# A chain of 270 weight blocks on one core: the first two blocks of a stage run on x·g, and the norm's factor is applied to their banks

## The chip, the cores and the metric

One core of a Trainium2 chip runs the whole program in one launch. The time is that of the device in microseconds (us): the median of three runs of the kernel before is 1714.77 (1704.56 to 1725.2). The engines are PE (matrix multiplication), ACT, DVE, POOL (GpSimd) and SP, which issues transfers. They run in parallel and meet at semaphores.

## The reference

Batch 1, 256 tokens, width 1024, all in fp32. Nine residual steps and two norms, each step on a normed x:

```
rmsnorm(x, g) = x * rsqrt(mean(x*x) + eps) * g
modulate(h, shift, scale) = h * (1 + scale) + shift        # shift, scale, gain from c_act @ mod_w + mod_b
swiglu(h) = (silu(h @ w_gate) * (h @ w_up)) @ w_out        # hidden width 2816
first model:  x += 0.5*swiglu(rmsnorm(x)); x += mixer_1(rmsnorm(x)); x += 0.5*swiglu(rmsnorm(x)); x = rmsnorm(x)
second model: for i in 0, 1:
    x += 0.5 * g1 * swiglu(modulate(rmsnorm(x), sh1, sc1))
    x += g2 * mixer(modulate(rmsnorm(x), sh2, sc2))        # i = 0: pool + SSD; i = 1: attention
    x += 0.5 * g3 * swiglu(modulate(rmsnorm(x), sh3, sc3))
return rmsnorm(x)
```

The mean runs over the 1024 channels of a token, so a norm needs the whole of x, while its factor is one number for each token.

## The kernel before

x is held transposed as 8 tiles of 128 channels by 256 tokens. The phases are n = 0 to 10: ffn, mix1, ffn, final norm (n = 3), ffn (4), mix2 (5), ffn (6), ffn (7), mix3 (8), ffn (9), final norm (10). All weights are one stream of 270 blocks of 128x2048 fp32 (1 MB), which SP loads into three slots in turn. ACT rounds a block to fp32r (`act_split`, L176, whi), DVE forms the remainder (`dve_split`, L184, wlo), and PE multiplies in three passes, hi by hi, lo by hi and hi by lo: 48 matmuls of 256 columns a block (`pe_in` L252, `pe_out` L284). x is treated alike: xh rounded by ACT, xl the remainder by DVE. Each slot is free again when PE has used it (semaphore w_used). F0 is a stage's first block. An ffn stage has 33 blocks: gate F0, up F0+1, then gate, up and out in turn, in loops on each engine. In the stages n = 0, 2, 4 and 6 DVE also works off the table of shifts and gains (`mod_block` L575, L578), which GpSimd loads; its sums end in a few PE matmuls before the last four output tiles of the stage (L504) and one DVE addition (L595).

Each engine does its instructions in the order in which they are written; nothing is reordered. Between two stages: DVE adds the output banks to x (`dve_residual` L304, or L309 with a gain, four pairs b = 0 to 3); ACT squares each pair (L335); DVE adds the two tiles of a pair (`dve_pair` L325); PE sums over channels with matmuls of one column (`pe_norm` L369) and runs matmuls without use between them (`pe_keep_warm` L357); ACT takes the square root (128x2, L340) and DVE the reciprocal (L391); PE spreads it over the partitions (L375); DVE forms xm = x·g·factor (`dve_norm` L401, 128x256 each, x8; in mix2 and mix3 also + shift, L398), ACT xh (L345, L347) and DVE xl (L428, L430). PE starts block F0 as soon as the first tile of xh is there (L244), the passes with xl last. The remainder of F0+1 is formed in two halves around the reciprocal (L222, L226). `post` multiplies silu(gate) by up (L532, L563, L534, L565).

## Time and profile before

| | us |
|---|---|
| median of three runs | 1714.77 |
| profiled execution, its own time | 1711.11 |
| its span (first to last instruction) | 1709.4 |
| PE busy in the span | 1675.8 |
| DVE busy | 1201.2 |
| ACT busy | 809.4 |
| POOL busy | 85.1 |

The page of the profile gives the busy time of each engine; the chain of waits follows the end of the program back, from each instruction to what released it. The mean granted clock of PE in this execution is 0.991 of full speed (2.4 GHz). Ends of matmuls are modelled, and PE counts as busy with the matmuls without use as well.

### The profile page before, as it was taken

The page shows a single profiled execution, that of the slowest core. Times are in us where ns is not written, and L with a number is a line of the kernel's source. Part 1 is how long each engine was busy: PE and PEld are TensorE (multiplying, and loading weights), DVE is VectorE, ACT ScalarE, POOL GpSimd, SP SyncE. Part 2 cuts the span into 40 slices and gives each one's busy share as a digit, 9 for nine tenths or more (in the row PEclk, how much of TensorE's full clock was granted, in tenths as well). Part 3 has the DMA queues.
Part 4 walks back from the last instruction along what each step waited for, and adds up shares of the span by engine and source line. Part 5 has one row for each costly group of instructions (what it writes and reads, how often), then busy time and mean ns, then how long its engine had stood idle before and what let it go on. Part 6 is the DMA issues. An engine that isn't in the chain of part 4 may idle for free.

```text
span 1709.4 us, 34392 instructions
## 1 busy us (share of the span) xinstructions
PE 1675.8 (98%) x14512; PEld 1641.4 (96%) x14512; DVE 1201.2 (70%) x1303; ACT 809.4 (47%) x874; POOL 85.1 (5%) x110
## 2 busy tenths in 40 slices
PE   9999999999999999999998999999999999999998
PEld 9999999999999999999997899999999988899998
DVE  5888875676788877878866778646555666764544
ACT  5444556644544344343565543435434455554342
POOL 0000000000000000000012000000000003100000
PEclk8999999999999999999999999999999999999999
DMA  7998754444498856888442368643555433345551
GB/s 311 344 340 308 265 176 171 147 150 164 176 347 325 326 214 230 318 323 304 177 149 102 122 249 320 242 175 138 208 203 189 170 123 128 126 168 191 179 196 50
DMA packets 50491, 365.08 MB, mean 214 GB/s; under 512 B 5728, under 2 KB 5856, under 8 KB 6240
## 3 DMA queue, kind: packets, MB, share of 16 engines
q1 hardware_dynamic: 39744, 287.04, 46.0%
q0 software_dynamic: 10368, 75.50, 11.9%
q8 instruction: 74, 1.21, 0.3%
q10 hardware_dynamic: 288, 1.18, 0.2%
q14 instruction: 17, 0.14, 0.0%
HBM read 362.65 MB, written 1.05 MB: 213 GB/s over the span
## 4 chain that ended last, share of the span: by engine, by line
PE 88%; DVE 7%; ACT 3%; issue 1%; DMA 0%; SPq 0%; ACTq 0%; DVEq 0%
PE bank L252 50%; PE bank L284 24%; PE bank L267 3%; PE bank L244 2%; DVE wlo L184 2%; PE bank L357 2%; PE bank L369 1%; PE bank L1661 1%; ACT whi L176 1%; DVE m_e L1923 1%; DVE m_p L1426 1%; ACT m_e L1802 0%; DVE xm L401 0%; DVE x L309 0%; PE bank L1619 0%
## 5 line engine op out<-in xcount | busy, mean ns | idle before, releaser
L184 DVE TENSOR_TENSOR wlo<-raw,whi 128x2048 fp32r<-128x2048 f32 x261 | 598.2, 2294 | 209.3 <-ACT whi L176 208.9
L252 PE MATMUL bank<-xh,whi 128*128 128x256 f32 x2608 | 729.6, 280 | 2.7 <-DVE wlo L184 1.4
L252 PE MATMUL bank<-xl,whi 128*128 128x256 f32 x2608 | 726.4, 279 | 0.0
L252 PE MATMUL bank<-xh,wlo 128*128 128x256 f32 x2608 | 726.3, 278 | 0.0
L176 ACT ACTIVATE whi<-raw 128x2048 fp32r<-128x2048 f32 x261 | 497.9, 1912 | 313.2 <-PE bank L252 187.4
L252 PEld LDWEIGHTS bank<-xh,whi 128*128 128x128 f32 x2608 | 492.2, 189 | 5.4 <-issue 2.8
L252 PEld LDWEIGHTS bank<-xh,wlo 128*128 128x128 f32 x2608 | 493.1, 189 | 0.0
L252 PEld LDWEIGHTS bank<-xl,whi 128*128 128x128 f32 x2608 | 490.4, 188 | 0.1
L284 PE MATMUL bank<-hid_hi,whi 128*128 128x256 f32 x1056 | 294.5, 279 | 0.0
L284 PE MATMUL bank<-hid_lo,whi 128*128 128x256 f32 x1056 | 294.1, 278 | 0.0
L284 PE MATMUL bank<-hid_hi,wlo 128*128 128x256 f32 x1056 | 294.1, 278 | 0.0
L284 PEld LDWEIGHTS bank<-hid_hi,wlo 128*128 128x128 f32 x1056 | 199.7, 189 | 0.0
L284 PEld LDWEIGHTS bank<-hid_hi,whi 128*128 128x128 f32 x1056 | 198.9, 188 | 0.4
L284 PEld LDWEIGHTS bank<-hid_lo,whi 128*128 128x128 f32 x1056 | 198.2, 188 | 0.0
L534 ACT ACTIVATE hid_hi<-hid 128x512 fp32r<-128x512 f32 x66 | 41.8, 633 | 283.1 <-DVE hid L563 283.1
L578 DVE SCALAR_TENSOR_TENSOR mod_acc<-mod_raw,c_act,mod_acc 128x1024 f32<-128x1024 f32 x126 | 161.6, 1282 | 2.6
L563 DVE TENSOR_TENSOR hid<-gate,bank 128x512 f32<-128x512 f32 x66 | 45.3, 686 | 81.9 <-PE bank L252 81.7
L1996 POOL DMA_DIRECT2D mod_raw<-mod_in x72 | 38.3, 532 | 937.0 <-DVE mod_acc L578 925.3
L565 DVE TENSOR_TENSOR hid_lo<-hid,hid_hi 128x512 fp32r<-128x512 f32 x66 | 45.7, 693 | 46.2 <-ACT hid_hi L534 46.2
L357 PE MATMUL bank<-ident_b 128*128 128x128 bf16 x690 | 49.5, 229 | 0.0
L357 PEld LDWEIGHTS bank<-ident_b 128*128 128x128 bf16 x690 | 46.7, 108 | 0.2
L659 DVE SCALAR_TENSOR_TENSOR m_pre<-bank,params,m_pre 128x255 f32<-128x255 f32 (+2 forms) x84 | 34.0, 474 | 14.9 <-ACT m_pre L646 14.9
(315 smaller groups left out, 1812.2 us busy)
## 6 DMA issues: line engine op xcount, KB each, us to landing
raw<-stream_in SPq DMA_DIRECT2D x270, 1024.0 KB, 4.8
mod_raw<-mod_in POOLq DMA_DIRECT2D x72, 1024.0 KB, 6.6
params<-params_in SPq DMA_DIRECT2D x1, 1474.0 KB, 16.0
x<-x_in SPq DMA_DIRECT2D x2, 512.0 KB, 4.4
...
```

Of the source, the lines that this page charges most:

```text
L176: act.activation(whi[:, s, :], raw[:, s, :], ACT.Copy).then_inc(sem("w_hi_ready"), 1)
L184: dve.tensor_tensor(wlo[:, s, :], raw[:, s, :], whi[:, s, :].bitcast(F32), ALU.subtract)\
L244: last = pe.matmul(out[:, m, :], w[:, s, c:c + P], (xh, xl)[part][:, k, :], start=(part == 0 and k == 0 and m == 0 and w is whi), stop=(pa ...
L252: last = pe.matmul(out[:, m, :], (whi, wlo)[wp][:, s, k * 256 + m * P:k * 256 + m * P + P], (xh, xl)[ap][:, k, :], start=(k == 0 and j == ...
L267: last = pe.matmul(out[:, tt, :], (xh, xl)[ap][:, k, tt * P:tt * P + P], (whi, wlo)[wp][:, s, k * 256:k * 256 + 256], start=(k == 0 and j ...
L284: mm = pe.matmul(pair(acc[d // 2])[:, d % 2, :], (whi, wlo)[wp][:, s, c:c + P], (hi, lo)[ap][:, kt, :], start=(first and d % 2 == 0 and kt ...
L357: pe.matmul(bank_[:, 0:P], ident_b[:, :], ident_b[:, :], start=True, stop=True, skip_group_check=True)
L534: act.activation(hid_hi[:, parity], hid[:, :, :], ACT.Copy).then_inc(sem("hid_rounded"), 1)
L563: dve.tensor_tensor(hid[:, :, :], gate[:, :, :], pair(UP), ALU.mult).then_inc(sem("hid_ready"), 1)
L565: dve.tensor_tensor(hid_lo[:, parity], hid[:, :, :], hid_hi[:, parity].bitcast(F32), ALU.subtract)\
L578: ins = dve.scalar_tensor_tensor(out=mod_acc[:, :], in0=mod_raw[:, s, t * D:t * D + D], scalar=c_act[:, k:k + 1], in1=mod_acc[:, :], op0=A ...
L1996: pool.dma_start(mod_raw[:, s, :], a_mod[ds(s * P + 2 * P * turn, P), :])\
```

## The change

In each of the nine stages with matmuls the first two blocks run on xg = x·g (and g·(1 + scale) where there is modulation), before the norm's factor is known. ACT rounds xg right after each pair of x (no instruction stood there before), and DVE forms its remainder between the pairs (`dve_scaled_rest`, L458 and L461). PE runs F0 and F0+1 on them (`pe_start`, L359); in the modulated stages each matmul has 258 columns: two more carry the shift. The squares are summed by GpSimd (`pool_squares`, L430 128x512 three times, L432 128x256) and by one fp32 matmul with a square of ones (L366) behind block F0; ACT takes a root of 128x256 (L413), DVE a reciprocal of 128x256 (L492). DVE then forms xm (L495), ACT xh, DVE xl (L504, L506), on which block F0+2 and all later ones run. The banks of the first two blocks are multiplied by the factor when DVE reads them (`dve_first_scaled`, L473), and the shift's column is copied first (L472). GpSimd forms the remainder of block F0+3 (`pool_split`, L448). The matmuls without use are gone but at the last norm. The norm between the models (n = 3) has no phase of its own any more: its factor and that of n = 4 are formed together in stage 4 (two ones matmuls, and GpSimd sums both sets of squares, L439), and x itself is normed late in that stage (`dve_final_inside`). A product of a pair stands one place later in the loops. SP issues half of params first, then x, the first block, consts and the next two blocks.

On DVE, from stage 6 to stage 7, the instructions before (L309 is the residual, L401 xm, L430 xl, L184 a block's remainder):

```order
L309 SCALAR_TENSOR_TENSOR x<-bank,gres,x 128x256 x2
L325 TENSOR_TENSOR xm<-xm 128x256
L457 SCALAR_TENSOR_TENSOR gmod<-mod_tab,params 128x8
L325 TENSOR_TENSOR xm<-xm 128x256
L222 TENSOR_TENSOR wlo<-raw,whi 128x1024
L391 RECIPROCAL rstd<-std 128x2
L226 TENSOR_TENSOR wlo<-raw,whi 128x1024
L401 SCALAR_TENSOR_TENSOR xm<-x,gmod,bank 128x256 x8
L423 TENSOR_SCALAR gres<-mod_tab 128x8
L430 SCALAR_TENSOR_TENSOR xl<-xm,mod_tab,xh 128x256 x8
L184 TENSOR_TENSOR wlo<-raw,whi 128x2048
L563 TENSOR_TENSOR hid<-gate,bank 128x512
```

and with the change (L288 is the residual, L461 the remainder of xg, L191 a block's remainder, L495 xm, L506 xl):

```order
L288 SCALAR_TENSOR_TENSOR x<-bank,gres,x 128x256 x2
L461 SCALAR_TENSOR_TENSOR xg_lo_a<-x,gmod,xg_hi_a 128x256 x2
L288 SCALAR_TENSOR_TENSOR x<-bank,gres,x 128x256 x2
L461 SCALAR_TENSOR_TENSOR xg_lo_a<-x,gmod,xg_hi_a 128x256 x4
L191 TENSOR_TENSOR wlo<-raw,whi 128x2048 x2
L492 RECIPROCAL rstd<-std 128x256
L495 SCALAR_TENSOR_TENSOR xm<-x,gmod,rstd 128x256 x8
L506 SCALAR_TENSOR_TENSOR xl<-xm,mod_tab,xh 128x256 x8
L513 TENSOR_SCALAR gres<-mod_tab 128x8
L609 SCALAR_TENSOR_TENSOR gmod<-mod_tab,params 128x8
L472 COPY cols<-bank 128x1
L473 TENSOR_TENSOR gate<-bank,rstd 128x256
```

The two whole remainders stand ahead of the reciprocal, which has 128x256 elements in the place of 128x2; reads of the four banks with the factor follow xl, and then the product of the first pair.

On PE, at the same place, before (L369 sums squares, L357 is the work without use, L244 the first block of stage 7):

```order
L369 MATMUL bank<-consts,xm 128x1
L357 MATMUL bank<-ident_b 128x128 x14
L369 MATMUL bank<-consts,xm 128x1 [waits x_paired]
L369 MATMUL bank<-consts,xm 128x1
L357 MATMUL bank<-ident_b 128x128 x8
L369 MATMUL bank<-consts,xm 128x1 [waits x_paired]
L369 MATMUL bank<-consts,xm 128x1
L357 MATMUL bank<-ident_b 128x128 x14
L375 MATMUL bank<-consts,rstd 128x128 [waits rstd_ready]
L375 MATMUL bank<-consts,rstd 128x128
L357 MATMUL bank<-ident_b 128x128 x26
L244 MATMUL bank<-xh,whi 128x256 [waits xn_rounded,w_lo_ready]
```

and with the change, around the matmul with ones (the rows ahead of it are the end of block F0, those behind it block F0+1):

```order
L359 MATMUL bank<-xg_hi_a,wlo 128x258 x2
L359 MATMUL bank<-xg_lo_a,whi 128x258 [waits xg_split]
L359 MATMUL bank<-xg_lo_a,whi 128x258
L366 MATMUL bank<-xm,consts 128x256 [waits squares_added]
L359 MATMUL bank<-xg_hi_a,whi 128x258 [waits w_lo_ready]
L359 MATMUL bank<-xg_hi_a,whi 128x258
L359 MATMUL bank<-xg_hi_a,wlo 128x258 x2
L359 MATMUL bank<-xg_lo_a,whi 128x258 x2
L359 MATMUL bank<-xg_hi_a,whi 128x258 x2
```

PE no longer waits for the reciprocal between the stages; it waits for GpSimd's sum of the squares between blocks F0 and F0+1.

On POOL, which before had only transfers in the ffn stages, the order of a stage is now:

```order
L2245 REGISTER_ALU
L2245 COMPARE_AND_BRANCH
L430 TENSOR_TENSOR xm<-xm 128x2x256 [waits x_squared]
L430 TENSOR_TENSOR xm<-xm 128x2x256 [waits squares_step,x_squared] x2
L432 TENSOR_TENSOR xm<-xm 128x256 [waits squares_step]
L448 TENSOR_TENSOR wlo<-raw,whi 128x2048 [waits w_lo_ready,w_hi_ready]
```

The fourth block's remainder stands behind the sums.

The diff, cut to its core:

```diff
-                if b >= 1 and n + 1 < len(phases):
-                    dve_pair(dve, n + 1, b - 1)
-            if n + 1 < len(phases):
-                dve_gain(dve, n + 1)
-                dve_pair(dve, n + 1, 3)
+                if b >= 1:
+                    dve_next_pair(dve, n, b - 1)
+            dve_next_pair(dve, n, 3)
...
+        def pe_start(pe, n):
+            F0, ni = first_block[n], split_index[n]
+            hi, lo = scaled_split(n)
+            w = width(n)
+            for b in range(2):
+                s = slot_of(F0 + b)
+                outs = [bank_[:, 0:w] for bank_ in first_banks(n)[b]]
+                pe.wait_ge(sem("w_lo_ready"), F0 + b + 1)
+                for k in range(KD):
+                    for j, (wp, ap) in enumerate(((0, 0), (1, 0), (0, 1))):
+                        if b == 0 and j == 0:
+                            pe.wait_ge(sem("xg_rounded"), 8 * ni + k + 1)
+                        if b == 0 and j == 2:
+                            pe.wait_ge(sem("xg_split"), 8 * ni + k + 1)
+                        for m in range(2):
+                            c = k * 256 + m * P
+                            last = pe.matmul(outs[m], (whi, wlo)[wp][:, s, c:c + P], (hi, lo)[ap][:, k, 0:w],
+                                             start=(k == 0 and j == 0), stop=(k == KD - 1 and j == 2), skip_group_check=True)
+                last.then_inc(sem("w_used"), 1)
+                if b == 0:
+                    if n == 0:
+                        pe.wait_ge(sem("consts_loaded"), 16)
+                    pe.wait_ge(sem("squares_added"), ni + 1)
+                    mm = pe.matmul(UP[:, 0:T], ones, xm[:, 0, :], start=True, stop=True, skip_group_check=True)
+                    if n == AFTER_FINAL:
+                        pe.wait_ge(sem("final_squares_added"), 3)
+                        mm = pe.matmul(UP[:, T:2 * T], ones, final_squares[:, 0, :], start=False, stop=True,
+                                       skip_group_check=True)
+                    mm.then_inc(sem("x_summed"), 1)
...
+            for b in range(4):
+                x_ready(act, n, b)
+                if b == 0 and shift is not None:
+                    act.activation(hi[:, :, T:W], pair_of_columns(shift), ACT.Copy)
+                for k in (2 * b, 2 * b + 1):
+                    act.activation(hi[:, k, 0:T], x[:, k, :], ACT.Identity, scale=g[:, k:k + 1]).then_inc(sem("xg_rounded"), 1)
+                if n > 0:
+                    squares(b)
...
+            act_split(act, F0 + 2)
+            act.wait_ge(sem("x_summed"), ni + 1)
...
+            act_split(act, F0 + 3)
...
+        def pool_squares(pool, n):
+            ni = split_index[n]
+            for b in range(1, 4):
+                pool.wait_ge(sem("x_squared"), 4 * ni + b + 1)
+                if b > 1:
+                    pool.wait_ge(sem("squares_step"), 3 * ni + b - 1)
+                pool.tensor_tensor(xm[:, 0:2, :], xm[:, 0:2, :], xm[:, 2 * b:2 * b + 2, :], ALU.add).then_inc(sem("squares_step"), 1)
+            pool.wait_ge(sem("squares_step"), 3 * ni + 3)
+            pool.tensor_tensor(xm[:, 0, :], xm[:, 0, :], xm[:, 1, :], ALU.add).then_inc(sem("squares_added"), 1)
+            if n == AFTER_FINAL:
+                fs = final_squares
+                pool.wait_ge(sem("final_squared"), KD)
+                for i, h in enumerate((4, 2, 1)):
+                    if i:
+                        pool.wait_ge(sem("final_squares_added"), i)
+                    pool.tensor_tensor(fs[:, 0:h, :], fs[:, 0:h, :], fs[:, h:2 * h, :], ALU.add)\
+                        .then_inc(sem("final_squares_added"), 1)
+        def pool_split(pool, n):
+            b = first_block[n] + 3
+            s = slot_of(b)
+            pool.wait_ge(sem("w_hi_ready"), b + 1)
+            pool.wait_ge(sem("w_lo_ready"), b)
+            pool.tensor_tensor(wlo[:, s, :], raw[:, s, :], whi[:, s, :].bitcast(F32), ALU.subtract)\
+                .then_inc(sem("w_lo_ready"), 1)
...
+        def dve_scaled_rest(dve, n, b):
+            ni = split_index[n]
+            hi, lo = scaled_split(n)
+            g = gain_of(n)
+            if b == 0 and n in MOD_OF:
+                dve.wait_ge(sem("xg_rounded"), 8 * ni + 1)
+                dve.tensor_tensor(lo[:, :, T:W], pair_of_columns(shift_of(n)), hi[:, :, T:W].bitcast(F32), ALU.subtract)
+            for k in (2 * b, 2 * b + 1):
+                dve.wait_ge(sem("xg_rounded"), 8 * ni + k + 1)
+                dve.scalar_tensor_tensor(out=lo[:, k, 0:T], in0=x[:, k, :], scalar=g[:, k:k + 1],
+                                         in1=hi[:, k, 0:T].bitcast(F32), op0=ALU.mult, op1=ALU.subtract)\
+                   .then_inc(sem("xg_split"), 1)
...
+        def dve_first_scaled(dve, n, b, outs):
+            F0, ni = first_block[n], split_index[n]
+            dve.wait_ge(sem("w_used"), F0 + b + 1)
+            for m in range(2):
+                bank_ = first_banks(n)[b][m]
+                if n in MOD_OF:
+                    dve.tensor_copy(cols[:, 68 + 2 * b + m:69 + 2 * b + m], bank_[:, T:T + 1])
+                dve.tensor_tensor(outs[m], bank_[:, 0:T], rstd[:, :], ALU.mult).then_inc(sem("first_scaled"), 1)
...
+            dve_split(dve, F0 + 2)
...
+            dve.reciprocal(rstd[:, :], std[:, :]).then_inc(sem("rstd_ready"), 1)
+            dve.wait_ge(sem("rstd_ready"), ni + 1)
...
+                dve.scalar_tensor_tensor(out=xm[:, k, :], in0=x[:, k, :], scalar=g[:, k:k + 1], in1=rstd[:, :],
+                                         op0=ALU.mult, op1=ALU.mult).then_inc(sem("xn_ready"), 1)
...
+            dve_gain(dve, next_stage(n))
+            dve.wait_ge(sem("w_lo_ready"), F0 + 4)
...
+            def first_post():
+                dve_first_scaled(dve, n, 0, [gate[:, m, :] for m in range(2)])
+                dve_first_scaled(dve, n, 1, [hid[:, m, :] for m in range(2)])
+                dve.wait_ge(sem("first_scaled"), 4 * split_index[n] + 4)
...
+            def turn(i, with_mod, last=False):
+                g0 = group0[f]
+                if with_mod:
+                    mod_block(0, g0, i)
+                dve_split(dve, F0 + 4, i, 6)
+                if with_mod:
+                    mod_block(1, g0, i)
+                dve_split(dve, F0 + 5, i, 6)
...
+            if n == AFTER_FINAL:
+                dve_final_inside(dve)
...
+            dve_split(dve, F0 + 34)
```

## Rows read from the trace of the kernel before

**Rows 1.** The page's first part: busy us of each engine, share of the span.
```profile
PE 1675.8 (98%) x14512; PEld 1641.4 (96%) x14512; DVE 1201.2 (70%) x1303; ACT 809.4 (47%) x874; POOL 85.1 (5%) x110
```

**Rows 2.** Busy time in the eight gaps between stages (span, then engines, granted clock, DMA).
```profile
437.98:443.43 5.45, 5.45 (x81) 5.44 (x82) 4.90 (x10) 1.88 (x5) 0.00 (x0) 1.00 0.00 0
625.20:640.82 15.62, 14.80 (x199) 14.55 (x198) 10.26 (x25) 5.22 (x12) 0.00 (x0) 0.89 0.20 69
...
1170.28:1176.27 5.99, 5.89 (x85) 5.71 (x83) 5.69 (x14) 2.24 (x5) 0.00 (x0) 1.00 0.02 3
...
sum 56.77, PE 54.63 PEld 53.42 DVE 48.77 ACT 19.24 POOL 0.00; mean PE 6.83 PEld 6.68 DVE 6.10 ACT 2.41 POOL 0.00
```

**Rows 3.** Chain of waits (start, us, what): stage 2's tables, then PE's blocks.
```profile
448.26 0.24 DVE tab_pos_f L1557
...
453.25 0.42 ACT cos L1581
...
455.64 11.32 PE bank L252 x96
...
686.20 11.31 PE bank L252 x96
...
834.37 6.91 PE bank L244 x48
```

**Rows 4.** Timeline of DVE from the end of stage 6 (last matmul 1170.28) on.
```profile
1170.71 0.87 DVE L309 SCALAR_TENSOR_TENSOR x<-bank,gres,x 128x256 f32<-128x256 f32 x2
...
1175.05 3.21 DVE L401 SCALAR_TENSOR_TENSOR xm<-x,gmod,bank 128x256 f32<-128x256 f32 x8
...
1178.25 3.25 DVE L430 SCALAR_TENSOR_TENSOR xl<-xm,mod_tab,xh 128x256 fp32r<-128x256 f32 x8
```

**Rows 5.** Groups of instructions of the whole program, by line.
```profile
L184 DVE TENSOR_TENSOR wlo<-raw,whi 128x2048 fp32r<-128x2048 f32 x261 | 598.2, 2294 | 209.3 <-ACT whi L176 208.9
...
L176 ACT ACTIVATE whi<-raw 128x2048 fp32r<-128x2048 f32 x261 | 497.9, 1912 | 313.2 <-PE bank L252 187.4
```

**Rows 6.** Timeline of DVE in mix1: a product with a bank, a reciprocal of 128x256.
```profile
292.32 0.42 DVE L980 TENSOR_TENSOR rstd<-std,bank 128x256 f32<-128x256 f32 x1 [1.20 <-ACT std L868]
292.77 1.75 DVE L982 RECIPROCAL rstd<-rstd 128x256 f32<-128x256 f32 x1
```

**Rows 7.** Timeline of POOL and DVE in mix2 (start, us; work that overlaps).
```profile
888.64 2.29 DVE L184 TENSOR_TENSOR wlo<-raw,whi 128x2048 fp32r<-128x2048 f32 x1 [1.89 <-ACT whi L176]
...
889.14 1.83 POOL L1385 COPY xm<-m_pu 128x4 f32<-128x4 f32 x1 [75.87 <-ACT m_pu L1294]
...
895.96 1.03 POOL L1386 TENSOR_TENSOR xm<-xm 128x504 f32<-128x504 f32 x1
895.98 3.16 DVE L184 TENSOR_TENSOR wlo<-raw,whi 128x2048 fp32r<-128x2048 f32 x1
...
906.75 2.38 POOL L1397 TENSOR_TENSOR xm<-xm,m_pu 128x1024 f32<-128x1024 f32 x1
```

**Rows 8.** Timeline of POOL and DVE in mix3, the same pair of engines.
```profile
1415.87 2.64 POOL L1848 TENSOR_TENSOR m_t<-m_qs,cos 96x512 f32<-96x512 f32 x1 [26.20 <-ACT m_qs L1832]
1417.28 0.68 DVE L1908 TENSOR_TENSOR m_qt<-bank,sin 96x512 f32<-96x512 f32 x1
...
1421.93 1.27 POOL L1848 TENSOR_TENSOR m_t<-m_qs,cos 96x512 f32<-96x512 f32 x1
```

**Rows 9.** Stretches of 2 us in mix2 with little work on PE, and the clock after.
```profile
910.00:912.00 2.00, 0.46 (x6) 0.27 (x4) 2.00 (x2) 1.22 (x3) 0.00 (x0) 1.00 0.00 0
...
914.00:916.00 2.00, 2.00 (x8) 1.67 (x8) 0.79 (x3) 0.73 (x2) 0.00 (x0) 0.50 1.00 422
```

**Rows 10.** The chain in mix3: sixteen fp32 matmuls of 256 columns.
```profile
1369.90 3.45 PE bank L1589 x16
```

**Rows 11.** The start: timeline of ACT (first rounding), chain of waits (block F0+4 begins).
```profile
9.51 1.06 ACT L212 ACTIVATE whi<-raw 128x1024 fp32r<-128x1024 f32 x1 [2.24 <-DMA raw<-stream_in]
...
41.73 5.44 PE bank L284 x48
```

More of the change, by code:

```diff
@@ L428, in dve_norm @@
+            if before_rest is not None:
+                before_rest()
+            for k in range(KD):
+                dve.wait_ge(sem("xn_rounded"), 8 * ni + k + 1)
+                if shift is None:
                     ins = dve.tensor_tensor(xl[:, k, :], xm[:, k, :], xh[:, k, :].bitcast(F32), ALU.subtract)
@@ new lines, in build_program, with pe_keep_warm, pe_norm @@
+        WARM = (14, 8, 14)
+        def pe_keep_warm(pe, count):
+            for _ in range(count):
+                pe.matmul(GATE[:, 0:P], ident_b[:, :], ident_b[:, :], start=True, stop=True, skip_group_check=True)
+        def pe_norm(pe, n):
+            ni = len(split_index)
+            for b in range(4):
+                if b == 0:
+                    pe.wait_ge(sem("silu_done"), STEPS * sum(kind == "ffn" for kind, _, _ in phases[:n]))
+                if b >= 2:
+                    pe_keep_warm(pe, WARM[b - 2])
+                pe.wait_ge(sem("x_paired"), b + 1)
+                for tt in range(2):
+                    mm = pe.matmul(STAT[:, T + tt:T + tt + 1], xm[:, 2 * b, tt * P:tt * P + P], ones[:, 0:1],
+                                   start=(b == 0 and tt == 0), stop=(b == 3), skip_group_check=True)
+            mm.then_inc(sem("x_summed"), 1)
+            pe_keep_warm(pe, WARM[2])
+            pe.wait_ge(sem("rstd_ready"), ni + 1)
+            for tt in range(2):
+                mm = pe.matmul(STAT[:, tt * P:tt * P + P], rstd[:, tt:tt + 1].to_broadcast([P, P]), ident,
+                               start=(tt == 0), stop=True, skip_group_check=True)
+            mm.then_inc(sem("rstd_spread"), 1)
@@ L509, in turn @@
                 for q in range(2):
-                    b = step(q, i)
+                    b = step(q, i, first and q == 0)
                     pe_out(pe, b, hid_hi[:, q], hid_lo[:, q], first and q == 0, False, i, 6)
@@ L1368, in act_mix2 @@
             round_heads(3)
-            for b in range(3, MIX2_OUT - 1):
+            for b in range(3, MIX2_OUT):
                 act_split(act, F0 + MIX2_IN + 2 + b)
-            act_split_halves(act, n + 1)
         def pool_mix2(pool):
@@ L2009, in turns @@
                             load(s, turn)
-                before = 2 * sum(MOD_GROUPS[f] for kind, f, _ in phases[:5] if kind == "ffn")
-                if len(phases) > 5:
-                    turns(1, before + 1)
-                    pool_mix2(pool)
-                    if before + 1 < 2 * N_GROUPS:
-                        turns(before + 1, 2 * N_GROUPS)
-                else:
-                    turns(1, 2 * N_GROUPS)
-            if any(kind == "mix3" for kind, _, _ in phases):
-                pool_mix3(pool)
+                done = 1
+                for n, (kind, f, _) in enumerate(phases[:-1]):
+                    if kind == "final":
+                        continue
+                    if n > 0:
+                        pool_squares(pool, n)
+                    pool_split(pool, n)
+                    if kind == "mix2":
+                        pool_mix2(pool)
+                    if kind == "mix3":
+                        pool_mix3(pool)
+                    if kind == "ffn" and MOD_GROUPS[f]:
+                        last = min(2 * (group0[f] + MOD_GROUPS[f]) + 1, 2 * N_GROUPS)
+                        turns(done, last)
+                        done = last
         @block.tensor
```

649 lines of the change are left out of this document (363 added, 286 removed).

## The prediction, made before the changed kernel was run

> **What bounds the kernel now.** I read the page's first part, then the windows of the stretches between stages, the chain of waits through them, and last the timelines of the engines there. PE is busy in 98% of the span [rows 1], so only what PE does can be shortened, or moved beside it. The windows show where it does no real work: in the eight gaps between stages it runs matmuls without use, and the gaps sum to 56.8 us, 15.6 of them round the norm between the models and 5.99 before stage 7 [rows 2]. Behind two gaps the first block is slow as well, 6.91 us in mix2 for a usual 5.65 [rows 3], and mix3's is alike, 1.3 each. In stage 2 the tables of angles (448.26 to about 453.7) hold up ACT, and block F0+2 begins at 455.64 [rows 3], 1.3 us later than two blocks of 5.44 behind the gap's end, 443.43 [rows 2], would give. So **about 61 us** are lost at stage boundaries, some 3.5%. The rest is 270 blocks at one of two paces, 5.65 us (half of 11.31) or 5.44 [rows 3, 11], and the little matmuls of the mixers.
>
> **The change, in the ffn stage 7.** Count from the last matmul of stage 6, at 1170.28. PE can now go on with F0 at once, since three of four pairs of x are ready by then. It does not wait again as long as remainders arrive: four blocks and the matmul with ones are the cover, 4 x 5.44 + 0.45 = 22.2 us, after which F0+4 needs its remainder. That matmul is my estimate: sixteen fp32 matmuls with 256 columns took 3.45 in mix3 for narrower weights [rows 10], two passes over 256 columns each make some 0.45.
>
> DVE's row up to the remainder of F0+4 is the path. Residual's last pair 0.8 (0.87 for two [rows 4]); four xg remainders behind it 1.6 and eight xm 3.2 (L401: 3.21 for eight [rows 4]); two block remainders 4.5 (2.29 each, a pitch of 2.25 [rows 5]); reciprocal 128x256 1.75 [rows 6] where one of 128x2 stood; eight xl 3.25 [rows 4]; gains 0.3; four reads of banks at 0.42 [rows 6] and four short copies, 1.9; the first product in two parts 0.8 (no such row; two of L401's kind); then ACT rounds the product, 0.7 (a quarter of a block's 1.91 and a start), and block F0+4, 1.9 [rows 5], and DVE forms its remainder, 2.3. The sum is 23.0 us. With nothing more it is 0.8 longer than the cover: a stall of about 1 us where 6 stood. ACT's own row (eight xg, four squares, two blocks, root, eight xh) lies beside this and is shorter. SP's transfers don't decide: slots come free in the same order as before, one block per 5.44 us, and in the gaps only 3 GB/s are moved now [rows 2].
>
> **GpSimd's part is not beside it.** In mix2 a GpSimd copy of 128x4 took 1.83 us: it began at 889.14 and ended with DVE's remainder (888.64 + 2.29). DVE's remainder took 3.16 in place of 2.29 when a GpSimd addition of 1.03 had begun 0.02 earlier [rows 7]. In mix3 a GpSimd product took 2.64 us for a usual 1.27 while DVE ran remainders, and a DVE product that reads a bank (0.68) was not held up beside it [rows 8]. So DVE work with both inputs in SBUF and GpSimd work exclude each other here. In the change nearly all of the row above is of that kind: xg, both block remainders, xm (its factor is now in SBUF, before it was in a bank), xl, the product. Only reciprocal and bank reads are free. What GpSimd does there is three adds of 128x512, 1.15 each (1.03 for 504 columns [rows 7], a bit more for the form with two rows), one of 256 columns 0.65, and the remainder of F0+3. The last is bounded by 2 x 2.29 (twice DVE's) and 2 x 2.38 (128x1024 twice [rows 7]); I take 4.5. Together 8.6, of which 1.75 can lie beside the reciprocal. What is left, 6.9, is added to DVE's row: **29.9 us for 22.2 of cover, a stall of 7.7** where the gap before had 5.99. Taking F0+3 from DVE (2.3) and giving it to GpSimd (4.5) makes the path longer by 2.2 if the two exclude each other.
>
> The Trainium skill has a rule on this, in "SBUF — State Buffer", section "Who interferes with whom": a DVE instruction with two SBUF inputs and a GpSimd instruction that reads SBUF share a port pair as a lock, held for the whole instruction by the one that issued first. The trace agrees, 1.83 for a copy of four columns and 3.16 for 2.29. For the length of GpSimd's fp32 addition of 2048 elements the "GPSIMD Engine Reference", section 3.1, has 4497 ns; by it the term stays what it is.
>
> **The other stages.** The same counting gives stalls for n = 1, 2, 4, 5, 6, 7, 8, 9 of 7, 12, 16, 9, 8.5, 8, 7, 7.5, together 75. Stage 2 has the tables' 5.0 us (448.26 to 453.25 [rows 3]) now within the row. Stage 4 has two sets of squares: GpSimd's adds of 1024, 512 and 256 columns (2.4 + 1.15 + 0.65) come before the ones matmuls, and PE waits about 8 us there, for a gap of 15.6 before; the 60 matmuls without use are gone, and x itself is normed late, where DVE has room (70% busy [rows 1]). Mixers have bank reads in other places but the same row up to F0+2. Against 61 before: **+14**. Ten matmuls with ones: **+4.5** (between stages there were only matmuls of one column). Two more columns in 258, in 12 blocks of 5.5 us: **+0.5**. The clock: PE idled about 1.5 us of 910 to 912, and at 914 to 916 its granted clock was 0.50, that is 1.2 GHz [rows 9]; it lasted some 3.5 us, so 1.75 lost. Stalls of 1.5 to 3 us come two or three to a boundary without warm matmuls. The bounds are none and 14 (one each at eight boundaries); I take three, **+5**, since most pieces are only about as long as that one. The start: the first rounding ends at 10.6, and F0+4 begins at 41.73 [rows 11]; by 10.6 + 29.9 it would be 40.5, **-1**. The last norm is as before, and a product that stands one place later in the loops still ends before its out block begins, a block of PE later: nothing; were that cover gone, it would show in every loop as a wait of PE for hid, some tenths of a us each.
>
> The sum is -1 + 14 + 4.5 + 0.5 + 5 = +23. On the profiled execution's own 1711.1 (its span is 1709.4), that is **1734 us**. The median of the runs shown is 3.7 above this execution, and runs spread over 20 us, which I read as stages falling on 5.44 or 5.65 (33 x 0.21 = 7 us a stage, at granted clock 1.00 both): the comparison moves by a few us for that alone. From the median as base it would be 1738; I keep 1734.
>
> **Rivals.** (a) *No lock, or GpSimd finds room* (chance 0.28). The row is 23.0; the stalls become 1 to 3 us, 6 in stage 2 and 8 in stage 4, together 27; that is 48 less. The start is then bound by PE's four blocks, partly at half clock, near 36.3, 4 less than above; few clock drops, 5 less: 1734 - 48 - 4 - 5 = **1677, faster**. It decides from the point where GpSimd's 6.9 us fit beside DVE: for it, there are only a few rows of exclusion, none with work as dense as here; against it, they show it in both directions, DVE held by GpSimd and GpSimd by DVE. (b) *GpSimd is kept out* (0.13): where DVE queues such work back to back, GpSimd waits until DVE comes to a reciprocal. No row shows this order. Sum of squares then ends 5 to 6 us late, PE waits for it before F0+1 with everything behind, and stalls are 9 to 11 us, 94 in all: +19, **1753, slower**. (c) *Half of the price* (0.17): GpSimd's additions fall between instructions or its work is shorter; stalls near 51, two or three us of clock: 1734 - 24 - 1 - 3 = **1706**. (d) The change may not do what it says only in stage 4, where the inner norm still waits; that is in the numbers.
>
> **How the numbers follow.** Forecast 0.42, (a) 0.28, (b) 0.13, (c) 0.17. A measurement tells about 1% from nothing: below 1697.6 faster, over 1731.9 slower. The forecast lies at that edge with ±12 around it (GpSimd's remainder 4.6 to 4.8 would add 1 to 2, clock 0 to 14, paces ±7): 0.24 slower, 0.17 within, 0.01 faster. (a) gives 0.26 faster and 0.02 within, (b) 0.13 slower, (c) 0.04 faster, 0.12 within, 0.01 slower. Faster 0.31, within 0.31, slower 0.38. The range is 1676 to 1756: it leaves out about half of (a) and a little of (b). The forecast's own range is 1720 to 1748.
>
> **What would show it.** The lengths of DVE's remainders and xm between F0 and F0+3: 2.3 and 0.47 alone, longer by GpSimd's work if it excludes them. GpSimd's remainder at 4.5, or longer and behind the others (then b). PE's waits before F0+1 (sum of squares), F0+2 (xl) and F0+4 (wlo): 2, 2 and 3 us by the forecast, only the last by (a), 6 in the first by (b). Granted clock below 0.9 in boundary windows for the clock's term. F0+4 of stage 0 at 40.5 or 36. I would be wrong on the path if PE waited for ACT there, or if the late work in stage 4 held up its loop.

## The result, and the profile after

Over 20 runs each, the changed kernel takes 1727.7 us (median; 1711.5 to 1747.25) and the kernel before 1715.34 (1699.39 to 1726.45). The ratio is 1.0074, 95% interval 1.0047 to 1.0102: 12.7 us slower by the ratio (12.4 by the medians), clear of zero and about 0.7%. Ratios are of fast runs alone, those within 1.5% of the fastest of their kernel, which leaves three of e5's ten runs out, its profiled one among them. The forecast was 1734 on a base of 1711.1, that is 23 us slower. The direction was right and so was the main mechanism, the size was 10 us too large.

The first part of the page after, against [rows 1]:

```profile
PE 1633.1 (95%) x13678; PEld 1592.5 (92%) x13678; DVE 1278.3 (74%) x1378; ACT 842.2 (49%) x958; POOL 182.6 (11%) x158
```

PE's busy time fell by 43 us, mostly because 690 matmuls without use became 36, and the span grew by 16: where PE ran those it now waits. DVE and POOL have 77 and 97 us more. Windows after (columns as in [rows 2]): the stretch from stage 6's last matmul to block F0+4 of stage 7; then four stretches with a wait or behind one (stages 2, 4, 6, 9).

```profile
1188.14:1218.09 29.95, 24.20 (x196) 23.00 (x195) 27.84 (x45) 18.31 (x28) 9.26 (x5) 1.00 0.28 106
476.00:488.00 12.00, 7.57 (x55) 7.61 (x56) 10.21 (x9) 5.82 (x5) 1.09 (x2) 0.72 0.58 212
...
651.00:660.00 9.00, 4.90 (x21) 4.72 (x22) 4.67 (x4) 3.00 (x4) 3.91 (x2) 0.50 0.55 212
...
1006.00:1012.00 6.00, 6.00 (x40) 5.91 (x39) 4.84 (x3) 2.78 (x3) 3.03 (x1) 0.76 0.41 158
1538.00:1544.00 6.00, 6.00 (x41) 6.00 (x40) 5.74 (x20) 3.48 (x7) 0.00 (x0) 0.72 0.33 138
```

29.95 us for four blocks, of which DVE is busy 27.84 and PE waits 5.8. The forecast row was 29.9. DVE's timeline in that stretch, the rows that answer to [rows 4] (start, us):

```profile
1188.17 0.87 DVE L288 SCALAR_TENSOR_TENSOR x<-bank,gres,x 128x256 f32<-128x256 f32 x2
1188.96 0.87 DVE L461 SCALAR_TENSOR_TENSOR xg_lo_a<-x,gmod,xg_hi_a 128x256 fp32r<-128x256 f32 x2
1189.75 0.87 DVE L288 SCALAR_TENSOR_TENSOR x<-bank,gres,x 128x256 f32<-128x256 f32 x2
1190.54 4.39 DVE L461 SCALAR_TENSOR_TENSOR xg_lo_a<-x,gmod,xg_hi_a 128x256 fp32r<-128x256 f32 x4
1194.85 4.48 DVE L191 TENSOR_TENSOR wlo<-raw,whi 128x2048 fp32r<-128x2048 f32 x2
1199.25 1.74 DVE L492 RECIPROCAL rstd<-std 128x256 f32<-128x256 f32 x1
1201.02 6.08 DVE L495 SCALAR_TENSOR_TENSOR xm<-x,gmod,rstd 128x256 f32<-128x256 f32 x8
1207.03 3.24 DVE L506 SCALAR_TENSOR_TENSOR xl<-xm,mod_tab,xh 128x256 fp32r<-128x256 f32 x8
```

and POOL's:

```profile
1189.59 4.28 POOL L430 TENSOR_TENSOR xm<-xm 128x512 f32<-128x512 f32 x3 [95.71 <-ACT xm L385]
1193.94 0.70 POOL L432 TENSOR_TENSOR xm<-xm 128x256 f32<-128x256 f32 x1
1199.47 4.58 POOL L448 TENSOR_TENSOR wlo<-raw,whi 128x2048 fp32r<-128x2048 f32 x1 [4.83 <-DVE wlo L191]
```

Read them side by side: four xg remainders, 1.6 us when alone, last 4.39 while GpSimd adds. Eight xm, 3.2 alone, last 6.08: GpSimd's remainder began 0.2 after the reciprocal, ran 1.55 beside it, and the other 2.9 are in xm's row. It lies so in stages 1, 2, 5, 7, 8 and 9; in 0, 4 and 6 it begins with xm, and all its 4.6 to 4.9 us are in xm's row. xl, behind it, has its usual 3.24 [rows 4]. The first two rows are two residual additions and two xg remainders that DVE still had to do after the last matmul (1188.14). What PE waits for in the whole execution (engine, line, waited for: us in total, times, longest):

```profile
PE bank L263 <- DVE wlo L191: 16.6, 6, 7.8
PE bank L223 <- ACT xh L420: 9.1, 6, 1.9
...
PE bank L359 <- DVE wlo L191: 7.6, 6, 1.3
PE bank L369 <- POOL final_squares L439: 7.5, 1, 7.5
...
PE bank L366 <- POOL xm L432: 4.7, 1, 4.7
```

The waits come where the forecast put them: before F0+1 (third row, 1.3 each, though for that block's remainder, which the lengthened xg work holds up, and not for the sum), at F0+2 for xh (1.9), and at F0+4 (7.8 in stage 2, with its tables). GpSimd's sum was waited for in one stage alone (4.7 us, stage 6).

**Where the time went, stage by stage.** Blocks have the two paces of [rows 3, 11], and which stage gets which differs from run to run, so spans of single runs can't be subtracted. I take the pace out: time from the last matmul of one stage to the last of the next, less its blocks at the mean spacing of their matmuls. What is left is waits, work without use, small matmuls (the mixers' own too) and lost clock; in mix3 (8) it also holds ten of the 18 blocks, whose matmuls have other shapes:

| beyond the blocks, us | 0 | 1 | 2 | 4 | 5 | 6 | 7 | 8 | 9 | sum |
|---|---|---|---|---|---|---|---|---|---|---|
| before | 20.3 | 38.7 | 7.6 | 16.9 | 50.7 | 6.5 | 6.8 | 103.8 | 6.6 | 257.8 |
| changed | 21.4 | 39.4 | 14.8 | 16.6 | 50.5 | 13.2 | 7.7 | 99.7 | 6.9 | 270.2 |

12.4 us more, as the runs have it. Two stages make it: 2 (+7.2) and 6 (+6.7). One gives back 4.1 (mix3), six stand within 1.2. For all versions I give this sum, and the time from the last matmul of the stage before to the first of block F0+4 (before, in stages 2, 4, 6, 7, 9: 29.0, 38.4, 28.7, 28.6, 29.3). Each sum is of one profiled execution, and mix2 (5) varies more than the others: 50.1 to 57.5 us over all versions, with a mean granted clock from 0.99 (changed) over 0.97 (before) and 0.94 (e3) to 0.92 (e8) in that stage. So a few us of a sum can be this alone.

### The profile page after: what moved, and what is told of

It is laid out like the page before. It is cut to its first block, busy times and chain, and to the rows that moved or that the text cites. A ratio compares the mean times of both kernels' runs of the same rounds, so it can differ in the third digit from the quotient of the medians.

```text
span 1725.5 us, 32891 instructions
## 1 busy us (share of the span) xinstructions
PE 1633.1 (95%) x13678; PEld 1592.5 (92%) x13678; DVE 1278.3 (74%) x1378; ACT 842.2 (49%) x958; POOL 182.6 (11%) x158
## 4 chain that ended last, share of the span: by engine, by line
PE 75%; DVE 17%; ACT 4%; issue 2%; POOL 1%; DMA 0%; DVEq 0%; SPq 0%; ACTq 0%; POOLq 0%
PE bank L231 43%; PE bank L263 23%; DVE wlo L191 4%; DVE xm L495 3%; PE bank L246 3%; PE bank L1877 2%; DVE xg_lo_a L461 2%; ACT whi L183 1%; DVE xl L506 1%; DVE rstd L492 1%; DVE x L288 1%; DVE m_p L1638 1%; DVE xl L504 0%; POOL final_squares L439 0%; PE bank L1888 0%
## 5 line engine op out<-in xcount | busy, mean ns | idle before, releaser
L191 DVE TENSOR_TENSOR wlo<-raw,whi 128x2048 fp32r<-128x2048 f32 x260 | 600.0, 2311 | 196.1 <-ACT whi L183 195.4
L183 ACT ACTIVATE whi<-raw 128x2048 fp32r<-128x2048 f32 x269 | 513.0, 1911 | 331.9 <-PE bank L231 179.7
L231 PE MATMUL bank<-xh,whi 128*128 128x256 f32 x2320 | 648.0, 279 | 2.4 <-DVE m_pre L852 2.4
L231 PE MATMUL bank<-xl,whi 128*128 128x256 f32 x2320 | 645.5, 278 | 0.0
L231 PE MATMUL bank<-xh,wlo 128*128 128x256 f32 x2320 | 645.4, 278 | 0.0
L231 PEld LDWEIGHTS bank<-xh,whi 128*128 128x128 f32 x2320 | 437.2, 188 | 4.2 <-DVE m_pre L852 2.8
L231 PEld LDWEIGHTS bank<-xh,wlo 128*128 128x128 f32 x2320 | 438.1, 189 | 0.0
L231 PEld LDWEIGHTS bank<-xl,whi 128*128 128x128 f32 x2320 | 435.6, 188 | 0.1
L263 PE MATMUL bank<-hid_hi,whi 128*128 128x256 f32 x1056 | 297.2, 281 | 16.6 <-DVE wlo L191 16.6
L430 POOL TENSOR_TENSOR xm<-xm 128x512 f32<-128x512 f32 x27 | 42.2, 1563 | 651.5 <-ACT xm L385 649.1
L2235 POOL DMA_DIRECT2D mod_raw<-mod_in x72 | 38.4, 534 | 537.2 <-DVE mod_acc L743 537.2
L359 PE MATMUL bank<-xg_hi_a,whi 128*128 128x258 f32 (+1 forms) x224 | 48.5, 299 | 13.0 <-DVE wlo L205 6.1
L359 PE MATMUL bank<-xg_lo_a,whi 128*128 128x258 f32 (+1 forms) x224 | 48.1, 297 | 3.3 <-DVE xg_lo_a L461 3.2
```

The costliest lines, as they stand in the source:

```text
L183: act.activation(whi[:, s, :], raw[:, s, :], ACT.Copy).then_inc(sem("w_hi_ready"), 1)
L191: dve.tensor_tensor(wlo[:, s, :], raw[:, s, :], whi[:, s, :].bitcast(F32), ALU.subtract)\
L231: last = pe.matmul(out[:, m, :], (whi, wlo)[wp][:, s, k * 256 + m * P:k * 256 + m * P + P], (xh, xl)[ap][:, k, :], start=(k == 0 and j == ...
L263: mm = pe.matmul(pair(acc[d // 2])[:, d % 2, :], (whi, wlo)[wp][:, s, c:c + P], (hi, lo)[ap][:, kt, :], start=(first and d % 2 == 0 and kt ...
L359: last = pe.matmul(outs[m], (whi, wlo)[wp][:, s, c:c + P], (hi, lo)[ap][:, k, 0:w], start=(k == 0 and j == 0), stop=(k == KD - 1 and j == ...
L430: pool.tensor_tensor(xm[:, 0:2, :], xm[:, 0:2, :], xm[:, 2 * b:2 * b + 2, :], ALU.add).then_inc(sem("squares_step"), 1)
```

## The experiments

All are made from the changed kernel; ratios are to the kernel before, with 95% intervals. The kernel before was run again beside each group, on the same chip: its median is 1714.3 for x1, x2, e3 and e4, 1709.4 for e5, e6 and e7, and 1716.0 for e8 and e9. Across groups the ratios can be compared, the times can't.

**x1: GpSimd's remainder on one column.** The rest of that remainder is left out.

```diff
-            pool.tensor_tensor(wlo[:, s, :], raw[:, s, :], whi[:, s, :].bitcast(F32), ALU.subtract)
+            pool.tensor_tensor(wlo[:, s, 0:1], raw[:, s, 0:1], whi[:, s, 0:1].bitcast(F32), ALU.subtract)
```

> The changed kernel, but GpSimd forms the remainder of block F0+3 for one column in place of 2048 (the rest of that remainder is left out, so its low part is missing from the product). Theory (GpSimd and DVE exclude each other; the 4.6 us of that remainder lie 1.7 beside the reciprocal and 2.9 in DVE's row): the eight xm of stage 7 take 3.2 us instead of 6.08, PE's row of a boundary gets 2.9 shorter, the wait for xl (1.8) goes and the wait for F0+4's remainder stays near 2; eight boundaries give some 20 us: about 1707. Rival 1 (GpSimd's work is beside DVE's and the row is long for its own instructions): xm stay at 6 us and the time stays at 1728. Rival 2 (its whole 4.6 us count): 8 x 4.6 = 37 less, 1691.

Measured: 1689.1 us, ratio 0.9882 (0.9814 to 0.9950). Beyond the blocks 244.9 in place of 270.2. DVE's timeline in stage 7, the eight xm:

```profile
1174.97 3.26 DVE L495 SCALAR_TENSOR_TENSOR xm<-x,gmod,rstd 128x256 f32<-128x256 f32 x8
```

POOL's timeline there:

```profile
1173.42 0.19 POOL L448 TENSOR_TENSOR wlo<-raw,whi 128x1 fp32r<-128x1 f32 x1 [4.83 <-DVE wlo L191]
```

xm went from 6.08 to 3.26 as forecast, F0+4 of stage 7 from 29.95 to 27.13 (-2.8). The sum fell by 25 where 20 was expected, the start giving 5 more. The time alone would not decide: it fell by some 33 us by the ratios, with four runs and an interval of 12 us to either side, which fits rival 2 (37) as well as 25. The rows decide: rival 1 needs xm at 6 us, and rival 2 needs 4.6 less at a boundary where 2.8 was measured. Part of the 33 can be pace (in the profiled execution one ffn stage is at 5.65, where the changed kernel's has three); the other three runs have no trace, so that isn't shown.

**x2: GpSimd's additions of squares on one column.** The sums of squares are left out.

```diff
-                pool.tensor_tensor(xm[:, 0:2, :], xm[:, 0:2, :], xm[:, 2 * b:2 * b + 2, :], ALU.add)
+                pool.tensor_tensor(xm[:, 0:2, 0:1], xm[:, 0:2, 0:1], xm[:, 2 * b:2 * b + 2, 0:1], ALU.add)
...
-            pool.tensor_tensor(xm[:, 0, :], xm[:, 0, :], xm[:, 1, :], ALU.add)
+            pool.tensor_tensor(xm[:, 0, 0:1], xm[:, 0, 0:1], xm[:, 1, 0:1], ALU.add)
```

> The changed kernel, but GpSimd's four additions of squares in each stage run on one column of 256 (the sum of the squares is left out, so the norms' factors are wrong). Its three additions on the second set of squares in stage 4 stay. Theory: the last four xg remainders before stage 7 take 1.6 us instead of 4.39, PE's wait before F0+1 (1.27) goes, the row gets 2.7 shorter, and stage 6, where PE waited 4.75 us for the sum, gains about 6; in all 7 x 2.7 + 6 = 25 less, about 1703. Rival (the additions run beside DVE's work and PE waits for the row in any case): same as the changed kernel, 1728.

Measured: 1722.4 us, ratio 1.0099 (1.0053 to 1.0145); beyond the blocks 273.2. The theory was wrong: the sum didn't fall, and the ratios of the two kernels lie within each other's intervals. DVE's timeline in stage 7:

```profile
1190.03 1.67 DVE L461 SCALAR_TENSOR_TENSOR xg_lo_a<-x,gmod,xg_hi_a 128x256 fp32r<-128x256 f32 x4
1191.61 4.48 DVE L191 TENSOR_TENSOR wlo<-raw,whi 128x2048 fp32r<-128x2048 f32 x2
1198.24 1.75 DVE L492 RECIPROCAL rstd<-std 128x256 f32<-128x256 f32 x1 [2.15 <-ACT std L413]
1200.03 7.58 DVE L495 SCALAR_TENSOR_TENSOR xm<-x,gmod,rstd 128x256 f32<-128x256 f32 x8
```

and POOL's, the third addition and the remainder of F0+3:

```profile
1191.71 4.44 POOL L430 TENSOR_TENSOR xm<-xm 128x2 f32<-128x2 f32 x1 [0.76 <-ACT xm L385]
...
1200.08 4.87 POOL L448 TENSOR_TENSOR wlo<-raw,whi 128x2048 fp32r<-128x2048 f32 x1 [3.67 <-ACT whi L183]
```

The xg remainders are back at 1.67, as forecast. But the third addition, two columns long, takes 4.44 us: it began 0.10 after DVE had begun its two block remainders and ended just behind both. That is what rival (b) of the prediction describes, GpSimd kept out while DVE queues such work. DVE then stands idle 2.15 us for its sum, and GpSimd's remainder, whose start hangs on ACT and the slot, no longer lies beside the reciprocal: all of it is in xm (7.58). In stage 1 of this run the same addition waited for one remainder only (2.17), the next addition for the other (2.12). In the changed kernel itself stage 6 shows it (POOL; the addition begins beside DVE's last xg remainder, 0.22 before the first of two block remainders, which run from 999.04 to 1003.52):

```profile
998.82 5.82 POOL L430 TENSOR_TENSOR xm<-xm 128x512 f32<-128x512 f32 x1 [1.18 <-ACT xm L385]
```

**e3: the remainder of F0+3 on DVE, behind xl.**

```diff
-            dve.wait_ge(sem("w_lo_ready"), F0 + 4)
+            dve_split(dve, F0 + 3)
...
-                    pool_split(pool, n)
```

> One part undone: DVE forms the remainder of F0+3, behind xl, GpSimd only sums squares. Theory: xm goes back to 3.2 us (-2.9), the remainder adds 2.25 to the same row ahead of F0+4's: -0.6 at each boundary, about 1722, not told from 1728 by the time, but xm, xl and the new remainder show it. Rival 1 (GpSimd's remainder was free): 2.25 x 8 = 18 slower, 1746. Rival 2 (its whole 4.6 counted): 8 x 2.3 = 19 faster, 1709.

Measured: 1719.1 us, 1.0038 (1.0003 to 1.0073); beyond the blocks 265.8, -4.4 where -5 was expected. That the sums agree is partly luck: mix2 is 4.6 up in this execution, the other stages together 9.0 down. DVE in stage 7:

```profile
1183.80 3.26 DVE L495 SCALAR_TENSOR_TENSOR xm<-x,gmod,rstd 128x256 f32<-128x256 f32 x8
1186.97 3.25 DVE L506 SCALAR_TENSOR_TENSOR xl<-xm,mod_tab,xh 128x256 fp32r<-128x256 f32 x8
...
1190.28 2.29 DVE L191 TENSOR_TENSOR wlo<-raw,whi 128x2048 fp32r<-128x2048 f32 x1
```

2.8 us less in xm, 2.25 more behind xl; F0+4 at 29.3 for 29.95. In stage 7 moving the remainder to GpSimd was worth nothing: it costs DVE 2.8 us to be rid of 2.25.

**e4: the squares summed by PE** with eight matmuls with ones; GpSimd keeps the remainder.

```diff
-                    pe.wait_ge(sem("squares_added"), ni + 1)
-                    mm = pe.matmul(UP[:, 0:T], ones, xm[:, 0, :], start=True, stop=True, skip_group_check=True)
+                    pe.wait_ge(sem("x_squared"), 4 * ni + 4)
+                    for k in range(KD):
+                        mm = pe.matmul(UP[:, 0:T], ones, xm[:, k, :], start=(k == 0), stop=(k == KD - 1),
+                                       skip_group_check=True)
...
```

> One part undone in another way: the squares are summed by PE with eight matmuls with ones (16 in stage 4) behind block F0, GpSimd adds nothing; it still forms the remainder of F0+3. Theory: DVE's row is 2.7 us shorter and still longer than PE's, which grows by 7 x 0.45 = 3.2 inside the stalls; so the boundary is 2.7 shorter, stage 6's 6, stage 4 about even (its wait of 7.5 for GpSimd becomes 15 x 0.45 = 6.7 of PE work): about 1703. Rival (PE's work is what counts): 8 x 3.2 + 6.7 = 32 slower less the waits of 1.27 and 4.75 to 7.5 removed, about 1740.

Measured: 1728.6 us, 1.0118 (1.0049 to 1.0186); beyond the blocks 271.9, +1.7. The theory's number was wrong by 25 us. As in x2, GpSimd's remainder no longer lies beside the reciprocal. POOL's timeline in stage 7:

```profile
1193.51 4.86 POOL L451 TENSOR_TENSOR wlo<-raw,whi 128x2048 fp32r<-128x2048 f32 x1 [110.21 <-ACT whi L183]
```

and DVE's:

```profile
1191.66 1.75 DVE L495 RECIPROCAL rstd<-std 128x256 f32<-128x256 f32 x1 [1.46 <-ACT std L416]
1193.45 7.58 DVE L498 SCALAR_TENSOR_TENSOR xm<-x,gmod,rstd 128x256 f32<-128x256 f32 x8
```

The reciprocal came 1.2 earlier against the last matmul of stage 6 (9.9 for 11.1), but GpSimd's remainder comes when ACT has rounded the block, just as the reciprocal is over, and now lies in xm whole: 7.58, for 6.08 in the changed kernel and 3.26 alone. So 1.2 gained and 1.5 lost, F0+4 at 30.3. Half a repair moved the exclusion to another place.

**e5: both, so that GpSimd does nothing at a boundary** (the edits of e3 and e4).

> The two undone parts together: the squares are summed by PE with eight matmuls, and DVE forms the remainder of F0+3 behind xl; GpSimd does nothing at a boundary. Theory: no instruction of DVE there is longer than alone (four xg remainders 1.66, eight xm 3.25, eight xl 3.25, remainders 2.25 apart); from the last matmul of stage 6 the reciprocal starts at 9.9, F0+4 at about 28.1 where it was 29.95 in the changed kernel and 28.7 in the kernel before. Against the changed kernel 8 x 1.5 less, about 1716; the row on DVE is then still longer than PE's four blocks and 3.6 us of sums. Rival (not the exclusion but the number of DVE's instructions is all that matters: one more remainder on DVE): 8 x 2.3 slower than the kernel with sums on PE alone, 1745.

Measured: 1713.8 us, 1.0011 (0.9968 to 1.0055); beyond the blocks 255.1, 15 under the changed kernel (by the ratios 11 less, 12 expected). F0+4 of stage 7 at 28.14 (28.1 expected). Neither e3 (-4.4) nor e4 (+1.7) gave it alone: together -15.1. Without mix2 the three are -9.0, -1.4 and -17.0, which says the same.

**e6: block F0+4 rounded before the first product** and its remainder between the product and hid_lo, on top of e5; in the loops of ACT and DVE the same block of the next turn then stands at a turn's end.

```diff
+            act_split(act, F0 + 4)
             first_post()
...
                 ins.then_inc(sem("hid_ready"), 1)
+                dve_split(dve, F0 + 4)
                 dve.wait_ge(sem("hid_rounded"), S0 + 1)
...
-                act_split(act, F0 + 4, i, 6)
                 act_split(act, F0 + 5, i, 6)
...
+                    act_split(act, F0 + 10, i, 6)
...
-                dve_split(dve, F0 + 4, i, 6)
...
+                    dve_split(dve, F0 + 10, i, 6)
```

> As the kernel without GpSimd's work, and block F0+4 of the ffn stages is rounded by ACT before the first product, and DVE forms its remainder between the product and hid_lo (before also the first work on the table of gains, which stood ahead of it). Theory: the tail from the bank reads to F0+4 (7.6 us) gets 1.5 to 2 shorter, F0+4 of stage 7 starts near 26.6 and PE's own work (four blocks, 3.6 of sums, 0.8 of small waits) is then the bound; six ffn stages gain 1.5 and three of them 2.6 more: about 1700. Rival (the bank reads and xl are the path, F0+4's remainder is not): 1716, as the kernel without it.

Measured: 1701.5 us, 0.9978 (0.9940 to 1.0015); beyond the blocks 244.6. From the last matmul of stage 6 (1169.0) to F0+4 of stage 7:

```profile
1169.00:1195.40 26.40, 26.35 (x211) 25.75 (x210) 24.64 (x46) 18.30 (x28) 0.00 (x0) 1.00 0.33 121
```

PE is busy 26.35 of 26.40 us: there is no wait left, only its own work, of which 3.6 are the sums. In stage 7 the theory holds (26.6 expected). Over the whole kernel the gain on e5 is smaller than the 16 that the theory had: 10.5 by the sums, 6 by the ratios.

**e9: the same with GpSimd's work kept** (the edit of e6 alone, on the changed kernel).

> The changed kernel with all of GpSimd's work kept, and only block F0+4's rounding and remainder taken ahead, as in the kernel e6. Theory: the tail of DVE's row gets 1.6 us shorter in six ffn stages and 2.6 more in stages 0, 4 and 6, 17 in all where the row is the bound: 1710. Rival (with GpSimd's work the wait sits at xl and the sum of squares, which this doesn't touch): 1724 to 1728.

Measured: 1714.9 us, 1.0003 (0.9978 to 1.0029); beyond the blocks 261.7, 8.5 less where 17 was expected (12 by the ratios). Stage 7 went from 29.95 to 27.97, and stage 6, though it kept its wait of 4.8 for GpSimd's sum, from 33.5 to 31.0. The six ffn stages give 12.0, and mix2 in this execution takes 2.9 back. The result lies between theory and rival: in stages 2, 7 and 9 the shorter tail gives 2.6, 2.1 and 2.0 for the 1.6 expected, in 0, 4 and 6 only 1.1, 0.9 and 3.3 for 4.2.

**e7 and e8: the tables of angles out of stage 2,** on top of e6. In e7 they stand behind the first product of stage 7, in e8 ahead of the last turn of its loop on DVE, and behind that turn on ACT (`TABLES_AT = 7` is in both; the call behind `first_post()` is e7's, the one ahead of `turn(4, ...)` e8's).

```diff
-TABLES_AT = 2
+TABLES_AT = 7
             first_post()
+            if n == TABLES_AT:
+                dve_tables(dve)
...
+            if n == TABLES_AT:
+                dve_tables(dve)
             turn(4, groups == 5, last=F0 + FFN_BLOCKS >= N_BLOCKS, end=True)
```

> As the kernel before it in this call, and the tables of angles are made in stage 7 behind the first product in place of the start of stage 2. Theory: stage 2 had 15 us of PE time beyond its blocks, the wait for F0+4's remainder 7.8 and half clock after it; it falls to about 6.5, like stages 7 and 9, and stage 7 stays under 6: about 1694, which is faster than the kernel before the change (1714) by 1.2%. Rival (the tables only move the wait to stage 7): 1700, as the kernel without it.

> As the kernel with early F0+4 and no GpSimd work at a boundary, with the tables of angles made by DVE in stage 7 ahead of its last turn of the loop, and read by ACT behind that turn. Theory: in the version with the tables behind the first product, stage 7 lost 10.2 us beyond its blocks in place of 3.7, because they stood ahead of F0+5's remainder (PE waited 4.4 for it, then ran a while at half clock); ahead of the last turn DVE has time, so stage 7 goes back to about 4 and stage 2 stays at 4: 6 us less, about 1694. Rival (a lump of 5 us on DVE is too long for three slots anywhere): PE waits there instead, 1700.

Measured: e7 1700.0 us, 0.9954 (0.9923 to 0.9984), beyond the blocks 242.5; e8 1704.5 us, 0.9943 (0.9917 to 0.9969), 238.9. In e7 stage 2 fell from 11.4 to 4.2, and stage 7 rose from 3.7 to 10.2: its rival came true, the tables only moved the wait. PE's waits for block remainders (whole execution: total, times, longest), e7, where the longest is stage 7's:

```profile
PE bank L231 <- DVE wlo L191: 7.8, 5, 4.4
```

and e8:

```profile
PE bank L231 <- DVE wlo L191: 3.0, 4, 1.0
```

In e8 both stages are at 4.2 and 4.0, as its theory had it. It is 0.6% under the kernel before, interval 0.3 to 0.8%, the lowest ratio here of a kernel that leaves nothing out; e7 can't be told from it. Its profiled execution gives 18.9 less beyond the blocks, its runs 9.8 less. In that execution mix2 is at 57.5 for 50.7 before: its mean granted clock was 0.92 in that stage (822.4 to 979.4), for 0.97 before.

| | beyond the blocks | F0+4 in stages 2, 4, 6, 7, 9 | ratio |
|---|---|---|---|
| before | 257.8 | 29.0, 38.4, 28.7, 28.6, 29.3 | 1 |
| changed | 270.2 | 35.2, 38.8, 33.5, 30.0, 29.3 | 1.0074 |
| x1 | 244.9 | 33.2, 34.5, 30.7, 27.1, 26.7 | 0.9882 |
| x2 | 273.2 | 35.5, 37.4, 30.7, 30.9, 30.0 | 1.0099 |
| e3 | 265.8 | 34.6, 36.7, 29.4, 29.3, 28.9 | 1.0038 |
| e4 | 271.9 | 36.0, 35.5, 31.0, 30.3, 30.2 | 1.0118 |
| e5 | 255.1 | 33.9, 33.4, 28.9, 28.1, 28.1 | 1.0011 |
| e6 | 244.6 | 31.0, 30.6, 26.2, 26.4, 26.1 | 0.9978 |
| e9 | 261.7 | 32.4, 37.5, 31.0, 28.0, 27.4 | 1.0003 |
| e7 | 242.5 | 26.2, 30.6, 26.4, 26.4, 26.3 | 0.9954 |
| e8 | 238.9 | 26.2, 30.8, 26.4, 26.4, 26.3 | 0.9943 |

## Why the prediction was right, and where its size was off

**The exclusion** of GpSimd and DVE was the step on which the sign hung, and x1, e3 and e5 show it: xm at 3.26 with GpSimd idle, 6.08 or 7.58 with it. The rule of the Trainium skill, "SBUF — State Buffer", "Who interferes with whom", that the two hold each other off for a whole instruction, fits these rows: reciprocals (1.74 beside a GpSimd remainder) and reads of banks (0.87 for two beside an addition) were not held up. Which of the two comes next did not follow the order of issue, as stage 6 below shows.

**The row on DVE** was forecast at 29.9 in stage 7 and measured at 29.95, but that close a hit is luck, since two errors cancel. Its single terms are the measured ones: reciprocal 1.75 (1.74), xl 3.25 (3.24), block remainders 4.5 (4.48), the product 0.8 (0.88), GpSimd's remainder 4.5 (4.58). But GpSimd put only 5.6 us into DVE's row (2.7 in xg, 2.9 in xm) where the forecast had 6.9. One reason stands in the rows: the first addition began beside residual reads of banks. And the forecast let the row start with the last residual pair, while DVE had 1.6 us of older work left at the last matmul, the two rows from 1188.17 to 1189.75.

**The term that was mis-sized is the difference per boundary**, +14 with +4.5 and +0.5. It compared a whole stall after with the gap before as the windows show it (56.8, about 61 with the slow blocks). Measured alike, from the last matmul to F0+4, stage 7 had 28.6 before, so 6.8 beyond four blocks of 5.44, not 5.99. What stands outside the window is block F0, a wait of 0.3 for the remainder of F0+3 and that block. From the chain of waits before:

```profile
1176.27 5.79 PE bank L244 x48
...
1193.25 5.70 PE bank L252 x48
```

Against 29.95 that is +1.4, where I had +2.6. In stage 9 it was 29.3 for 29.3 (forecast +2.3), in stage 4 +0.5 (+1.5). Only part of this is the gap before: less four blocks at each stage's own pace, stages 7, 9 and 4 had 6.8, 6.7 and 15.8 before, for 6.0, 5.8 and 15.6 in the forecast, and 8.2, 6.7 and 16.2 after, for 8.6, 8.1 and 17 (the forecast's stalls with the matmuls with ones and the wider columns). So the stall after was too large too, by 0.4 to 1.4. The stages 1, 4, 5, 7 and 9, which went as planned, came to +1.6 together beyond the blocks, where the forecast's terms make 10. That is most of the error; the others (mix3 -4.1, stage 2 +1.3, stage 6 +3.3, the clock, counted apart from them, -5, and the start +2.1) come to about -2 together.

**Mix3** was forecast even and gave 4.1 back: its own chain of small steps starts 3.7 us earlier after the boundary (its long row of matmuls at L1661, now L1877, begins 50.5 us after the last matmul of the stage before, for 54.1). Some of it is clock: the mean granted clock of the stage was 0.99 before and 1.00 after, with 0.57 over 1394 to 1398 before. The prediction followed the mixers only to F0+2, and no run here takes that stage apart, so the cause of the rest stays open.

**Stage 6** was forecast at +3.4 and is +6.7: there rival (b) came true within the forecast's own case. GpSimd's third addition began 0.22 before DVE's two block remainders, ended behind both (5.82 us), and PE waited 4.7. GpSimd's remainder then fell past the reciprocal, and xm took 7.61 for 6.08 in stage 7; the chain of waits has it:

```profile
1008.91 7.61 DVE xm L495 x8
```

I had treated the two orders as one property of the whole run; they go stage by stage, by tenths of a microsecond. **Stage 2** was forecast +5.9 with its tables, and is +7.2 with the clock: granted 0.72 over 476 to 488, and 1.00 in all of that stage before. e7 and e8 show that it is the tables: in e6 the stage has 11.4, without them 4.2.

**The clock** was +5 for three falls, and the windows show it low in stages 2, 6, 9 and, behind the wait for the two sums, 4. In stage 7 the waits, 5.8 us in all and none over 1.8, left it at 1.00; in stage 9 waits of 3.8 us in all, none over 1.8 either, came before 0.72 over 1538 to 1544. Its size can be estimated from the mean granted clocks of the two executions, 0.991 over 1709 us and 0.987 over 1726: 15 and 22 us of full clock lost, some 7 more, if PE had work all that time. That fits the +5, but other executions differ (mix2 above), and the sums beyond the blocks hold this cost. **The start** was forecast -1 and is +1.1: F0+4 at 41.66, not 40.5; there GpSimd's remainder began behind the reciprocal, so none of it lay beside that; x1 takes 3.7 off, e3 1.4, so GpSimd's work is in that row as well. Sum: boundaries +11.3 measured, clock in it, start +1.1, for +19, +5 and -1.

**The rivals.** (a), no exclusion, is out. (b) is out as a rule, and right in stage 6. (c) would have been 5 us faster than its base, and its reason, cheaper GpSimd work, was not found: 4.28 + 0.70 + 4.58, waits included, for 8.6 forecast. Yet its direction was: DVE paid 5.6 of the 6.9. The measured +12.7 lies between (c) and the forecast, nearer the forecast, whose own range (1720 to 1748) holds 1727.7; the stated range of 1676 to 1756 was so wide because of (a).
